# Attention of a transformer block: outputs in two PSUM banks by turns, turned probabilities in two banks in place of three

## The reference

```python
# branch B ("forgetting"): causal, with a bias from the running sum of gates
logit = einsum('bqhd,bshd->bhqs', q_blk, kb) * ATTN_SCALE
logit = logit + cq - cum_t                       # bias per key
logit = where(causal, logit, NEG_INF)
p = softmax(logit);  o = einsum('bhqs,bshd->bqhd', p, vb)

# branch A ("sparse"): the top 256 keys of an indexer, one key head for all
logit = einsum('bqhd,bqkd->bqhk', q_blk, k_sel) * ATTN_SCALE
logit = where(valid, logit, NEG_INF)
p = softmax(logit);  o = einsum('bqhk,bqkd->bqhd', p, v_sel)
```

## Time and profile before

| | us |
|---|---|
| median of 3 runs | 1652.07 (1651.61 to 1652.73) |
| the profiled execution, its own time | 1651.5 |
| its span, first to last instruction | 1649.6 |
| TensorE busy | 1532.6 (93%) |
| VectorE busy | 846.3 (51%) |
| ScalarE busy | 508.6 (31%) |
| attention, first transpose to last output copy | 543.9 to 781.0 |
| score matmuls (line 1342), idle before them | 79.3, 6.8 |
| transposes (line 1355), idle before them | 80.2, 4.3 |
| value matmuls (line 1367), idle before them | 77.0, 7.2 |

### The profile page before, as it was taken

How to read it: one execution, slowest core, us unless ns; L and a number is a source line. 1 busy time by engine, 2 the same in 40 slices (tenths; PEclk the granted TensorE clock), 3 DMA queues, 4 the chain that set the end, 5 groups by cost and what they waited for, 6 DMA issues and landing times.

```text
span 1649.6 us, 23994 instructions
## 1 busy us (share of the span) xinstructions
PE 1532.6 (93%) x8440; PEld 935.4 (57%) x8441; DVE 846.3 (51%) x1981; ACT 508.6 (31%) x1044; POOL 205.9 (12%) x372
## 2 busy tenths in 40 slices
PE   6999999999999999998999993899999999999992
PEld 3565578789889666666887871333333333333330
DVE  6786887997887677776666545111111111111113
ACT  4326711122212677777222221111111111111113
POOL 0110000000000121000000001122222222222221
PEclk9999999999999999999999995999999999999996
DMA  9650223332211000202576239999899459998995
GB/s 367 217 175 3 88 82 133 96 116 52 52 44 34 27 27 1 78 1 83 177 238 226 85 111 383 369 401 342 311 379 413 119 182 341 403 403 335 414 394 211
DMA packets 122233, 326.32 MB, mean 198 GB/s; under 512 B 14814, under 2 KB 64006, under 8 KB 97570
## 3 DMA queue, kind: packets, MB, share of 16 engines
q1 hardware_dynamic: 110404, 308.36, 49.6%
q0 software_dynamic: 11744, 16.82, 4.5%
HBM read 301.74 MB, written 34.39 MB: 204 GB/s over the span
## 4 chain that ended last, share of the span: by engine, by line
PE 85%; DVE 6%; DMA 4%; issue 2%; ACT 2%; SPq 1%; POOL 0%; POOLq 0%; ACTq 0%; DVEq 0%
PE ps L1487 21%; PE ps L1213 11%; PE ps L1215 11%; PE ps L1214 11%; PE ps L1505 10%; PE ps L1342 4%; PE ps L1355 3%; PE ps L1167 3%; PE ps L1367 3%; DVE arena L1806 2%; DMA arena<-in_w_e_up_dram 2%; DMA arena<-in_w_mod_dram 2%; PE ps L1200 1%; PE ps L1481 1%; PE ps L1170 1%
## 5 line engine op out<-in xcount | busy, mean ns | idle before, releaser
L1487 PE MATMUL ps<-arena 128*64 128x512 f32 x1632 | 374.3, 601 | 13.3 <-issue 9.4
L1487 PEld LDWEIGHTS ps<-arena 128*64 128x64 f32 x1632 | 114.2, 138 | 226.8 <-issue 215.5
L2118 DVE TENSOR_TENSOR arena<-arena,ps 128x256 f32<-128x256 f32 x51 | 21.5, 421 | 403.2 <-ACT arena L1083 403.2
L1505 PE MATMUL ps<-arena 128*64 128x512 f32 x816 | 183.8, 592 | 0.6 <-DVE arena L2134 0.6
L1751 DVE TENSOR_SCALAR_CACHE_REDUCE arena<-arena,small 128x384 bf16<-128x384 f32 (+2 forms) x192 | 169.6, 941 | 0.0
L1213 PE MATMUL ps<-rounded_quad,rounded_pair 128*128 128x512 f32 x352 | 138.5, 393 | 1.3 <-ACT arena L895 1.3
L1215 PE MATMUL ps<-rounded_quad,rounded_pair 128*128 128x512 f32 x352 | 137.1, 390 | 0.0
L1214 PE MATMUL ps<-rounded_quad,rounded_pair 128*128 128x512 f32 x352 | 137.1, 390 | 0.0
L808 POOL DMA_INDIRECT sum_rows<-arena,ones x51 | 81.4, 1597 | 403.1 <-DVE arena L2134 393.9
L1806 DVE CUSTOM_DVE_ANT_0 arena<-ps,arena 128x896 f32<-128x896 f32 (+7 forms) x128 | 91.8, 755 | 70.2 <-PE ps L1342 69.6
L1505 PEld LDWEIGHTS ps<-arena 128*64 128x64 f32 x816 | 58.8, 137 | 116.5 <-issue 116.5
(11 more groups left out here) (314 smaller groups left out, 2421.6 us busy)
## 6 DMA issues: line engine op xcount, KB each, us to landing
arena<-in_w_e_up_dram SPq DMA_DIRECT2D x64, 1024.0 KB, 17.1
arena<-in_w_e_gate_dram SPq DMA_DIRECT2D x64, 1024.0 KB, 14.5
arena<-in_w_e_down_dram SPq DMA_DIRECT2D x32, 2048.0 KB, 14.2
arena<-in_w_mod_dram SPq DMA_DIRECT2D x12, 2048.0 KB, 9.6
plain_pair<-in_w_in_dram SPq DMA_DIRECT2D x30, 512.0 KB, 5.2
arena<-in_x_dram SPq DMA_DIRECT2D x16, 512.0 KB, 7.5
gate_rows<-arena SPq DMA_DIRECT2D x16, 512.0 KB, 3.6
arena<-gate_rows SPq DMA_DIRECT2D x32, 256.0 KB, 3.4
```

Of the source, the lines that this page charges most:

```text
L1487: m = pe.matmul(ps[o * TB:(o + 1) * TB, 2, 0:2 * FQ].rearrange("p (j n) -> p j n", j=2), xT[:, k % NX, k // NX * TB:(k // NX + 1) * TB], w ...
L1505: m = pe.matmul(ps[o * TB:(o + 1) * TB, 5, 0:DQ], hidT[:, k % NH_T, k // NH_T * TB:(k // NH_T + 1) * TB], w_dn[c][:, k, o * DQ:(o + 1) * D ...
```

## The change

The unit's output goes to bank 6 or 5 by turns (`out_bank`), in the matmuls and in the copy; the values of unit n wait for the output copy of unit n-2, not n-1. The turned groups use banks 7 and 4 by turns; group k waits for the copy of group k-2, not k-3. TensorE's order in a step is now two groups of transposes, the scores three ahead, and then the rest of the groups. No instruction that computes is added or taken away.

```diff
 def turn_bank(k):
-    return (7, 4, 5)[k % 3]
+    return (7, 4)[k % 2]
+
+def out_bank(n):
+    return (6, 5)[n % 2]
...
-                if k >= 3:
-                    pe.wait_ge(pt_copied, k - 2)
+                if k >= 2:
+                    pe.wait_ge(pt_copied, k - 1)
...
-                if f == 0 and n >= 1:
-                    pe.wait_ge(o_done, n)
+                if f == 0 and n >= 2:
+                    pe.wait_ge(o_done, n - 1)
...
-                        m = pe.matmul(ps[z * HD:(z + 1) * HD, 6, 0:P], v, pT[k % PT][:, (2 * i + z) * P:(2 * i + z + 1) * P],
+                        m = pe.matmul(ps[z * HD:(z + 1) * HD, out_bank(n), 0:P], v, pT[k % PT][:, (2 * i + z) * P:(2 * i + z + 1) * P],
...
-                for f in range(min(groups, 3)):
+                for f in range(min(groups, 2)):
                     turn_p(n, f)
                 if n + LEAD < N_U:
                     scores(n + LEAD)
-                for f in range(3, groups):
+                for f in range(2, groups):
                     turn_p(n, f)
...
-                dve.tensor_copy(oT[kind == "b"][p][:, b * P:(b + 1) * P], ps[:, 6, 0:P]).then_inc(o_done, 1)
+                dve.tensor_copy(oT[kind == "b"][p][:, b * P:(b + 1) * P], ps[:, out_bank(n), 0:P]).then_inc(o_done, 1)
```

## The result

The changed kernel takes 1659.72 us (median of 4 runs, 1657.35 to 1660.23), the kernel before beside it 1651.84 (4 runs). The ratio is 1.0034 with a 95% interval of 1.0018 to 1.0049: slower by 3 to 8 us. The two medians are 7.9 us apart, near the upper end of that interval. The forecast was 1659.0, or +6.9.

The account below looks back on a forecast made before the run. The prediction took TensorE, busy 93% of the span, as the bound; its place-by-place terms in attention summed to +6.9 us, 1658.4 for the profiled execution, forecast as 1659.0 us, with a range of 1652.5 to 1665.0.

Parts of the forecast that it names:

- the prediction's own signs of being wrong: Transposes' wait near 3.5 us, scores' wait down by more than 2, or attention and whole span giving different sums.
- each of three forgetting periods: Returns from query block 0 to 7: late ScalarE copies delay turned groups, +0.92 us each, +2.8; three-group units add 0.15 each.
- change of kind: Between forgetting and sparse kinds: the 0.40 us output wait goes, the fourth group's extra 0.51 takes it back: 0.
- last, with the tail: In the tail, waits of 2.04 and 0.48 us go whole and about 0.3 comes back: -2.2.
- What bounds the kernel: TensorE, busy 93% of the span: a microsecond gained or lost in attention should arrive at the kernel's end.
- Outputs in two banks: Values before the output copy: all ten waits for the preceding unit's copy, 6.2 us, are exposed and removed.
- part two: Turned probabilities in two banks: three-group units gain a change of work; group k waits for the copy of k-2.
- Turned groups in two banks: Where ScalarE's copies come late, each large unit pays 0.51 us; sparse b=4 units +0.83 each; free ScalarE costs nothing.
- The change of work, 0.15: Twelve three-group units with a free ScalarE switch kinds of TensorE work once more, 0.15 us each: +1.8.
- Rival A: Large attention units: first ScalarE copy always early enough, every bank-6 wait a gain: -3.8 us, 1648.3; chance 0.08.
- Rival B: Scores issued one group (0.44 us) earlier take back 4.0 us in nine late units: +2.9, 1655.0; chance 0.20.
- Rival C: Copies late in all 32 units of three and four groups: +12.5 us, 1664.6; chance 0.10.

Follow-up runs that it names:

- two_turn_banks: Changed kernel with outputs in bank 6 alone, turned groups still in two banks: attention 247.2 us, whole 1.0045 of the kernel before.
- order_alone: Kernel before with only the new TensorE order (two groups, scores, rest) and its old banks: attention 238.4 us, whole 1.0000 of before.
- out_early: Kernel before with VectorE's output copy moved ahead of the division: attention 234.1 us, whole 0.9972 of before.
- split_exp_before: Kernel before with ScalarE's copies of the first two groups between the two heads' exponentials: attention 235.7 us, whole 0.9994 of before.
- split_exp_after: Changed kernel with ScalarE's copies of the first two groups between the two heads' exponentials: attention 235.3 us, whole 0.9971 of before.
- out_early_split: Kernel before with output copy ahead of the division and first two ScalarE copies between the exponentials: attention 227.6 us, whole 0.9939 of before.
- old_order: Changed kernel with up to three groups of transposes ahead of the scores, as before: attention 272.9 us, whole 1.0230 of the kernel before.
- both_orders_after: Changed kernel with output copy ahead of the division and first two ScalarE copies between the exponentials: attention 235.2 us, whole 0.9973 of before.

## Why the prediction was right

The forecast was +6.9 us in attention, and +6.0 was measured. That the whole came out as close as 1659.0 to 1659.72 is in part luck: attention was forecast 0.9 too high, and the profiled execution has 2.8 us more outside attention (1.1 ahead, 1.7 behind), which the forecast put at nothing. By the letter one of the prediction's own signs of being wrong appeared with that, for attention gives +6.0 and the span +8.8; the last section shows that the part behind attention comes with falls of the granted clock that don't follow the banks, and the part ahead differs by up to 3.2 us between profiles. The terms of the sum, rounded and grouped by places that start with the scores of a block 7:

| stretch | forecast | measured, before and after |
|---|---|---|
| start of attention to the first such scores | +0.9 | +0.8 (19.24, 20.07) |
| each of three forgetting periods | +1.2 | +1.15 (30.32, 31.47) |
| change of kind | +0.25 | +0.1 (27.65, 27.79) |
| second sparse period | +1.5 | +1.45 (29.36, 30.81) |
| third, with the modulation step | +1.2 | +0.9 (30.76, 31.69) |
| last, with the tail | -0.7 | -0.8 (40.53, 39.73) |

- **What bounds the kernel.** Right: attention's +6.0 arrived; the stretch behind it didn't give any back, and was 1.7 longer itself.
- **Outputs in two banks.** The waits went whole, and most of them, 0.41 at each return and 0.64 in block 4, lay under the wait that part two brings. Two_turn_banks shows that: 2.7 us of 6.2. The Trainium skill (Perfetto Trace Analysis, Optimizing Tensor Performance, Matmuls) asks for banks in rotation so that the copy out of one overlaps the next matmuls; by two_turn_banks the rule is worth 2.7 us on the outputs, and what it costs to take a bank from the turned groups is 8.8 (247.2 less the 238.4 of order_alone, which has the same order). The same page (Identifying Performance Opportunities, Optimization Strategy) says that gaps which repeat can mean too few buffers; out_early and split_exp_before show the other cause, since the same banks lost those gaps to an order.
- **Turned groups in two banks.** A copy start frees the bank 0.62 us later, and the fourth group goes about half a microsecond after the third. At the return I expected the third group 0.63 us after a copy start and found 0.62; in block 4 of the sparse kind I charged +0.83 and scores to values took 6.60 us where they took 5.75 (from block 7's scores, 687.29 to 693.89 and 681.76 to 687.51), +0.85; in block 7 I charged 0.51 and found 0.48 (1.07 for 0.59).
- **The change of work, 0.15.** Right where it was charged: block 5 of the first period takes 2.46 us from transposes to values where it took 2.30. Order_alone shows that this is not the whole account of the order, since it returns as much in the sparse kind with three banks.
- **Rival A** (ScalarE never late) gave -3.8 us from a copy that starts 0.2 us earlier at the return and 1.3 us in the sparse kind. The rows named say otherwise, and the trace after has those late copies again (609.62 and 692.89), so the premise was false. Its number is not confirmed: split_exp_after has early copies and lies 3.2 below before, but 2.8 of that is what ScalarE's order gives the kernel before by itself. Between the two kernels with early copies the change gives -0.4, with 2.2 us of waits for ScalarE and 1.8 more before the scores that A didn't count.
- **Rival B** (scores a group earlier give half back) fits order_alone; in the changed kernel the scores' wait rises from 6.8 to 8.6 us and the loss is nearly whole. **Rival C** is excluded by twenty waits, not thirty-two at full price.

## What to carry to other kernels

A wait for a buffer is not yet a case for a second buffer: look first at what the releasing instruction stands behind in its engine's queue. Here both waits (3.5 and 6.2 us) came from a place in a queue, and two reorderings on two engines took 10.9 us off attention, while moving a bank from one wait to the other, with the order that goes with it, cost 6.0. When two engines take turns to be late, an edit that cures one shows only part of its gain, so try both together; and work out what is late next at each place, for seven of the ten waits removed here were under another one.

## What was not expected of the hardware

The 1.7 us behind attention. Groups of 16 router matmuls (line 1435 before, 1440 after), with the granted clock of the same stretches from the windows view (stretch; TensorE, weight loads, VectorE, ScalarE, GpSimd busy; clock, DMA share, GB/s). Before:

```profile
980.65 1.95 PE L1435 MATMUL ps<-arena 128*128 128x36 f32 x16 [1.11 <-ACT arena L1065]
...
980.00:982.40 2.40, 1.75 (x16) 1.78 (x17) 2.32 (x5) 0.99 (x3) 1.17 (x8) 1.00 0.22 87
984.00:988.00 4.00, 3.44 (x16) 3.29 (x16) 0.32 (x3) 1.59 (x2) 0.00 (x0) 0.50 1.00 264
```

After:

```profile
989.00 3.53 PE L1440 MATMUL ps<-arena 128*128 128x36 f32 x16 [1.11 <-ACT arena L1070]
...
989.00:992.30 3.30, 3.30 (x16) 3.30 (x17) 2.32 (x5) 0.34 (x1) 1.75 (x11) 0.51 0.08 32
```

The granted clock falls from 1.00 to 0.50, that is from 2.4 to 1.2 GHz, at this place in both kernels, ahead of the routing in which TensorE mostly idles. Before, it fell behind the group shown (1.95 us at 1.00; the next group ran at 0.50), after, it fell ahead of it: the same 16 matmuls took 3.53 us. From its start to the start of the next transposes it is 1.77 us before and 3.33 after. TensorE had been idle for about a microsecond ahead of the group in both profiles, so the traces don't say why it fell earlier in one.

The 1.7 us are a balance of three pieces, measured from the first projection matmul. The first transposes ahead of the router start 120.1 us behind it before and 121.3 after, +1.2: TensorE waits 3.88 us for VectorE in both (to 873.59 and 880.73), the clock falls to 0.50 behind that wait, and over the same 20 us its mean is 0.91 before and 0.83 after. The first matmul after the routing (line 1460 before, 1465 after) starts at 214.1 and 217.4, so the router adds 2.0 or so. The first matmul of line 1505 (1510 after) starts at 257.1 and 258.9, so 1.5 come back at the start of the expert stage.

Neither fall follows the banks. Over the ten profiles the mean clock at the first place is 0.91 in six and 0.83 in four, order_alone, with the banks of before, among the four. In the router the clock fell ahead of this group in the changed kernel and two_turn_banks, ahead of the next group in before, split_exp_before, out_early and out_early_split, and behind both in order_alone, old_order, split_exp_after and both_orders_after, of which the last three have the changed kernel's banks. The stretch behind attention was between 867.2 and 869.2 us over all ten, with no edit in it. What sets the moment of the fall stays open: one profile of each kernel was read.
